# Rotary pairs exchanged by DMA, and the delta rule's chunk inverse with T as transposes of two heads

## The reference

```python
# delta rule, per chunk (kernel: chunks of 128, so that each has two 64-row halves)
m = where(strict, einsum('ik,jk->ij', kb, kc) * decay, 0)
t_mat = triangular_solve(eye + m, eye)                 # inverse of a unit lower triangular matrix
u = t_mat @ vb - (t_mat @ (kb * exp(gcum))) @ state
o = (qc * exp(gcum)) @ state + ((qc @ kc.T) * decay) @ u
state = state * cd + kd.T @ u
# retention: rotary position on q and k, then causal scores with a decay
x * cos(phase) + rotate_every_two(x) * sin(phase)      # rotate_every_two: (-x2, x1) for each pair (x1, x2)
o_ret = ((q @ k.T) * d_mat) @ v
```

## Time and profile before

| | |
|---|---|
| median of 3 runs | 1973.21 us (1970.41 to 1974.37) |
| profiled execution | 1973.4 us |
| its span | 1971.1 us |
| TensorE busy | 1950.8 us, 99% |
| VectorE, ScalarE, GpSimd busy | 1034.0, 757.2, 89.3 us |
| mean granted clock of TensorE | 0.995 |

### The profile page before, as it was taken

One profiled execution on the slowest core, in us unless ns is written; L12 is line 12 of the kernel. 1 busy time (PEld: TensorE's weight loads), 2 busy tenths in 40 slices (PEclk: granted clock), 3 DMA queues, 4 the chain that ended last, 5 costly groups with the idle time before them and its releaser, 6 DMA issues.

```text
span 1971.1 us, 26542 instructions
## 1 busy us (share of the span) xinstructions
PE 1950.8 (99%) x10157; PEld 1558.7 (79%) x10157; DVE 1034.0 (52%) x1416; ACT 757.2 (38%) x936; POOL 89.3 (5%) x81
## 2 busy tenths in 40 slices
PE   8999999999999999999999999999999999999999
PEld 6778888888888788877888888887777788888887
DVE  7745655676447667565543334236668454323433
ACT  5472243445324344443432124134555443212312
POOL 0020210100000010000100000020000010000001
PEclk9999999999999999999999999999999999999999
DMA  6222012232332243212332232342322032223221
GB/s 231 85 88 83 27 36 73 86 101 75 102 107 85 67 139 106 70 59 68 104 107 85 88 104 85 106 126 84 102 80 84 22 107 95 97 85 106 85 93 56
DMA packets 146166, 176.95 MB, mean 90 GB/s; under 512 B 3485, under 2 KB 140317, under 8 KB 143904
## 3 DMA queue, kind: packets, MB, share of 16 engines
q1 hardware_dynamic: 143008, 160.44, 24.9%
q0 software_dynamic: 2784, 15.06, 2.5%
q10 hardware_dynamic: 288, 0.26, 0.0%
HBM read 173.55 MB, written 2.20 MB: 89 GB/s over the span
## 4 chain that ended last, share of the span: by engine, by line
PE 96%; DVE 2%; ACT 1%; issue 0%; DMA 0%; DVEq 0%; ACTq 0%
PE bank L806 28%; PE bank L807 28%; PE bank L808 28%; PE bank L927 3%; PE bank L1394 2%; PE bank L1411 1%; PE bank L961 1%; PE bank L933 1%; PE bank L921 1%; DVE w_lo L1491 1%; PE bank L1215 1%; PE bank L1268 1%; PE bank L969 1%; PE bank L1007 0%; PE bank L999 0%
## 5 line engine op out<-in xcount | busy, mean ns | idle before, releaser
L806 PE MATMUL bank<-n_hi,w_hi 128*128 128x512 f32 x1504 | 612.0, 407 | 7.5 <-DVE w_lo L1507 6.4
L807 PE MATMUL bank<-n_lo,w_hi 128*128 128x512 f32 x1504 | 597.8, 398 | 0.0
L808 PE MATMUL bank<-n_hi,w_lo 128*128 128x512 f32 x1504 | 592.8, 394 | 0.0
L1486 ACT ACTIVATE w_hi<-raw 128x2048 fp32r<-128x2048 f32 x152 | 291.3, 1916 | 766.7 <-PE bank L808 764.3
L1491 DVE TENSOR_TENSOR w_lo<-raw,w_hi 128x2048 fp32r<-128x2048 f32 x152 | 349.3, 2298 | 282.6 <-ACT w_hi L1486 280.7
L806 PEld LDWEIGHTS bank<-n_hi,w_hi 128*128 128x128 f32 x1504 | 283.0, 188 | 85.0 <-issue 15.3
L806 PE MATMUL bank<-ff_hi,w_hi 128*128 128x512 f32 x848 | 338.1, 399 | 3.7 <-DVE ff_lo L2543 2.1
L807 PE MATMUL bank<-ff_lo,w_hi 128*128 128x512 f32 x848 | 338.0, 399 | 0.0
L808 PEld LDWEIGHTS bank<-n_hi,w_lo 128*128 128x128 f32 x1504 | 282.7, 188 | 67.6
L807 PEld LDWEIGHTS bank<-n_lo,w_hi 128*128 128x128 f32 x1504 | 283.2, 188 | 66.7 <-issue 5.3
L808 PE MATMUL bank<-ff_hi,w_lo 128*128 128x512 f32 x848 | 334.6, 395 | 0.0
(11 more groups left out here) (334 smaller groups left out, 1529.4 us busy)
## 6 DMA issues: line engine op xcount, KB each, us to landing
raw<-in_mlp_w_in SPq DMA_DIRECT2D x32, 1024.0 KB, 5.5
raw<-in_mlp_w_out SPq DMA_DIRECT2D x32, 1024.0 KB, 4.9
raw<-in_w_up SPq DMA_DIRECT2D x22, 1024.0 KB, 5.1
raw<-in_w_units SPq DMA_DIRECT2D x14, 1024.0 KB, 4.5
raw<-in_a_w_qkv SPq DMA_DIRECT2D x12, 1024.0 KB, 5.2
raw<-in_b_w_qkv SPq DMA_DIRECT2D x12, 1024.0 KB, 5.2
b_bias<-bias_table POOLq DMA_DIRECT2D x16, 448.0 KB, 4.7
raw<-in_w_down SPq DMA_DIRECT2D x8, 768.0 KB, 4.2
```

Of the source, the lines that this page charges most:

```text
L806: nc.tensor.matmul(b[:, :], w_hi[:, j % 2, cols], hi, start=start, stop=False)
L807: nc.tensor.matmul(b[:, :], w_hi[:, j % 2, cols], lo, start=False, stop=False)
L808: return nc.tensor.matmul(b[:, :], w_lo[:, j % 2, cols], hi, start=False, stop=final)
L1486: act.activation(w_hi[:, s, :], raw[:, s, :], ACT.Copy).then_inc(hi_ready, 1)
```

## The change

1. **Pairs by DMA.** The turn matrix goes; sine has its sign by the row's parity. GpSimd issues four DMAs that copy odd to even rows and even to odd rows of the queries' and keys' tiles into `turned`, now `proj[:, 24:32]`. GpSimd's cosines go; VectorE does sine, cosine and sum of all 8 tiles, 4 before the copies of `p_ret[2]` and 4 behind them (`rotated`).
2. **T by transposes.** In levels 1 to 5 a chunk's T is two full 128x128 transposes, each of two heads' blocks of both halves (`corners_turned`). So T of head h comes to lie in the rows of half h % 2, and so must P. From level 2 on, P and Z are issued for two chunks in two banks, with all four 64x64 tiles (`crossed_products`). In level 6 P goes to the rows by h % 2, and Z is issued crossed.
3. **Order.** T of chunks 2 and 3 moves behind P of chunks 0 and 1 of the next level. The key-query products move from before `p_ret[3]` into levels 1 to 4; values 0 and 1 are transposed within `p_ret[3]`, keys 0 behind A0. In the state loop the four scores are spread: one before u, one behind it, two behind ds. ScalarE's split of weights and its gates move behind T of levels 3 and 4. `g_Y` moves to the buffer of `g_X`, and the copies to it wait until the blocks are placed.

```diff
@@ the ring's list
-        for name in ("gram", "qk"):
-            ring += [(name, c) for c in range(TOK)]
-        ring += [("rot", n) for n in range(4)]
-        ring += [("A0", c) for c in range(TOK)]
+        ring += [("gram", c) for c in range(TOK)] + [("vt", 0), ("vt", 1)]
+        ring += [("A0", c) for c in range(TOK)] + [("kt", 0)]
...
-        LEVEL_BESIDE = {1: [("kt", 0), ("rot", 4)], 2: [("kt", 1), ("rot", 5)], 3: [("kt", 2), ("rot", 6)],
-                        4: [("rot", 7), ("vt", 0)], 5: [("vt", 1)], 6: [("vt", 2), ("vt", 3)]}
+        LEVEL_BESIDE = {1: [("qk", 0)], 2: [("kt", 1), ("qk", 1)], 3: [("kt", 2), ("qk", 2)],
+                        4: [("qk", 3)], 5: [("vt", 2)], 6: [("vt", 3)]}
@@ mixer_pool
+            for half in range(2):
+                group_left(pool, p_ret[half], 1)
+                pool.wait_ge(at("l2_scaled"), 4 * half + 4)
+                for row in range(2):
+                    pool.dma_start(turned[row::2, 4 * half:4 * half + 4, :], proj[1 - row::2, 16 + 4 * half:20 + 4 * half, :]).then_inc(
+                        at("pairs_turned%d" % half), 16)
@@ TensorE
+        def crossed_products(pe, name, n, two, parts, cols, lhsT, rhs):
+            b = [ring_group(pe, (name, n, 2 * two + k)) for k in range(2)]
+            for c in (2 * two, 2 * two + 1):
+                for pair in range(2):
+                    for i, (h, half) in enumerate(parts):
+                        h += 2 * pair
+                        if name == "P":
+                            k, rows = half, HALVES[h % 2]
+                        else:
+                            k, rows = h % 2, HALVES[half]
+                        at0 = (2 * (c % 2) + pair) * cols
+                        ins = nc.tensor.matmul(b[k][rows, at0:at0 + cols], lhsT(c, h, half), rhs(c, h, half), start=True, stop=True)
+                        if c % 2 and pair and i >= len(parts) - 2:
+                            ring_filled(ins)
...
+            for pair in range(2):
+                ins = nc.tensor.transpose(b[:, pair * P:(pair + 1) * P], src[:, 2 * pair:2 * pair + 2, :].rearrange("p h d -> p (h d)"), ident)
@@ mixer_tensor
                 for c in range(TOK):
+                    if c == 2 and n > 1:
+                        corners(n - 1, (2, 3))
...
+                            two_taken(pe, "Z", n - 1, c)
+                            crossed_products(pe, "P", n, c // 2, ((0, 0), (1, 1), (1, 0), (0, 1)), SIDE // 2,
+                                             lambda c, h, half: g_m[HALVES[half], c, h, HALVES[half]],
+                                             lambda c, h, half: odd_blocks(g_Y[:, c], n)[HALVES[half], h])
...
+                        two_taken(pe, "P", n, c)
+                        two_taken(pe, "T", n - 1, c)
+                        rows_of_T = lambda c, h, half: g_T[HALVES[h % 2], c, h // 2 * 2 + half, :]
+                        if n < last:
+                            crossed_products(pe, "Z", n, c // 2, ((0, 0), (1, 0), (0, 1), (1, 1)), SIDE // 2, rows_of_T,
+                                             lambda c, h, half: g_P[HALVES[h % 2], c, h // 2 * 2 + half, 0:SIDE // 2])
...
+                    corners(n, (0, 1))
...
+                retention_scores(pe, c, (1,))
                 ring_taken(pe, ("vt", c))
...
-                retention_scores(pe, c)
+                retention_scores(pe, c, (0,))
...
+                retention_scores(pe, c, (2, 3))
                 pe.wait_ge(at("qd_ready"), c + 1)
@@ VectorE
+        def rotated(dve, half):
+            dve.wait_ge(at("pairs_turned%d" % half), 32)
+            for n in range(4 * half, 4 * half + 4):
+                q = proj[:, 16 + n, :]
+                dve.tensor_tensor(turned[:, n, :], turned[:, n, :], const("sin"), ALU.mult)
+                own_dve(dve, dve.tensor_tensor(q, q, const("cos"), ALU.mult))
+                done(dve, dve.tensor_tensor(q, q, turned[:, n, :], ALU.add), at("rope_done"), n + 1)
...
+            rotated(dve, 0)
             copies(dve, p_ret[2], 24, lambda: grams_vector(dve))
-            key_queries_vector(dve)
+            rotated(dve, 1)
             first_inverse(dve)
-            copies(dve, p_ret[3], 28, lambda: turned_vector(dve, range(4)), leave=True)
+            copies(dve, p_ret[3], 28, lambda: [values_beta(dve, c) for c in range(2)], leave=True)
```

More of the change, by code:

```diff
@@ L275, in build @@
             ("a_pT", [P, 4, SEQ], F32))
[L277 removed]
+        spent = CONST_AT["far_lower"][0]
         a_vn = consts[:, spent:spent + 15 * P].rearrange("p (c d) -> p c d", c=5)
@@ L526, in build @@
         BANKS.update({name: tuple(range(8)) for name in MIXER_RING})
-        BANKS.update({("rot", n): tuple(range(8)) for n in range(4, 8)})
+        BANKS.update({("qk", c): tuple(range(8)) for c in range(TOK)})
+        BANKS.update({key: (4, 5, 6, 7) for key in (("vt", 0), ("vt", 1), ("kt", 0))})
         BANKS.update({key: (4, 5, 6, 7) for key in [("A0", c) for c in range(TOK)] + [("ro", 2), ("ro", 3)]})
@@ L566, in ring_taken, with two_taken, two_chunks @@
             eng.wait_ge(free, before + 1)
+        def two_taken(eng, name, n, c):
+            for k in range(2):
+                ring_taken(eng, (name, n, c // 2 * 2 + k))
+        def two_chunks(v, two, k):
+            return v[:, 2 * two:2 * two + 2, k::2, :].rearrange("p c x d -> p (c x) d")
         def banks_left(eng, banks, key):
@@ L982, in grams, with key_queries, values_turned_first, retention_scores @@
                 four_products(pe, ("gram", c), lambda h: chunk(4 + h, c), lambda h: chunk(4 + h, c))
[L984 to L995, removed]
+        def key_queries(pe, c):
+            four_products(pe, ("qk", c), lambda h: chunk(4 + h, c), lambda h: chunk(h, c))
+        def values_turned_first(pe):
+            pe.wait_ge(at("silu_v"), 1)
+            for c in range(2):
+                four_transposes(pe, ("vt", c), lambda h: chunk(8 + h, c))
+        def retention_scores(pe, h, parts):
             pe.wait_ge(at("rope_done"), 8)
-            for j in range(TOK):
+            for j in parts:
                 b = ring_group(pe, ("rs", h, j))
@@ L1050, in mixer_tensor @@
                 if n < last:
-                    for c in range(TOK):
-                        ring_taken(pe, ("Z", n, c))
-                        side_turned(pe, ("T", n, c), g_Y[:, c], HALVES if n < last - 1 else HALVES[0:1])
+                    corners(n, (0, 1))
             for c in range(TOK):
@@ L1846, in retention, with side @@
                 ring_done(act, act.activation(proj[:, 16 + h, :], b[:, :], ACT.Copy), ("ro", h))
-            def side(b, rows, cols=4 * SIDE):
-                return b[rows, 0:cols].rearrange("p (h d) -> p h d", h=4)
+            def side(b, rows, n=4):
+                return b[rows, 0:n * SIDE].rearrange("p (h d) -> p h d", h=n)
             def key_decayed(c):
```

151 lines of the change are left out of this document (70 added, 81 removed).

## The result

| | before | changed kernel |
|---|---|---|
| runs, median | 1971.81 us (1969.93 to 1974.37, 4 runs) | 1954.32 us (1952.93 to 1956.53, 4 runs) |
| profiled execution, time and span | 1973.4 and 1971.1 us | 1953.94 and 1951.4 us |
| instructions of TensorE | 10157 | 9893 |

The ratio is 0.9909, with a 95% interval of 0.9896 to 0.9923: 17.5 us faster between the medians. Forecast were 11.9 us. Of the 7.2 us, 5.6 are gain that was not forecast; the other 1.6 come from the starting point, a profiled execution of 1973.4 us where the median of the four runs before is 1971.81.

What follows compares the result with a forecast made beforehand. TensorE, 96% of the chain, was taken as the bound. A0 6.05 us earlier, then levels 29.56, waits 0.4 and level 6 4.3, put the inverse's first product 11.9 earlier: 1973.4 - 11.9 = 1961.5 us, range 1957.5 to 1968.

Steps and rivals of the forecast that it cites:

- Ahead of the inverse: Last projection up to level 1: turn and key-query products leave, values' transposes enter; A0 starts 6.05 us earlier, at 211.96.
- The wait of 0.25 us: Head of level 1: TensorE, ready at 214.4, waits 0.25 us for VectorE's last copy of the projection, at 214.65.
- The exchange by DMA: Pairs copied SBUF to SBUF on GpSimd's queue before the rotations: costs 0 us, with 4 kept as possible lateness.
- both of my bounds: First DMA pair: at double the row's 5.2 us it costs nothing; at four times it lands 4 us late.
- T as transposes: Levels of the inverse: T in four chunks falls from 1.90 to 1.16 us, two excursions of 0.58.
- My 0.14 us: Price of TensorE going from 64x64 tiles to 128 and back, 0.58 less 0.44; 10 excursions for T, 1.4 us.
- The levels: Levels 1 to 5 of the inverse: P and Z keep instruction counts at 29.5 ns each; 29.56 us together.
- rival 1: P and Z of levels 2 to 5: crossed tiles take turns at 61 ns, +16.1, in all 1977.6 us; chance 0.03.
- Rival 2: Inverse: the clock falls to half, tile instructions about 53 ns, +18 and +10 us, so 1989; chance 0.03.
- Rival 3: Level ends, head of level 1 or first exchange: waits eat part of the gain, 1963.5 to 1968.5 us; chance 0.25.
- Rival 4: Inverse: switches cost less, level 6 runs at 3.5, no waits: -14 us, 1959.5; chance 0.08.
- The state loop: Behind the inverse: reordered scores remove a wait of 0.38 us but bring three of 0.15; sum 0.

Runs made afterwards that it cites:

- behind_z: The changed kernel with the group beside each level moved behind Z, in front of T of the first two chunks; 1954.68 us, ratio 0.9912.
- eight_in_turn: The changed kernel with the 32 instructions of each crossed two-chunk group sorted by tile, eight in succession on each; 1972.08 us.
- pairs_alone: The kernel before with only the exchange of pairs by DMA, key-query products and inverse as before; 1968.37 us, ratio 0.9978.
- t_by_products: The changed kernel with T as crossed 64x64 products with the identity, 32 per two chunks, in place of four full transposes; 1960.17 us.
- old_inverse: The changed kernel with P, T and Z as before: two tiles, T by products, one bank per chunk; 1963.83 us, ratio 0.9965.

## Why the prediction was right in sign and too small

Point by point, by its own steps:

- **Ahead of the inverse**: right. A0 was forecast at 211.96 and came at 212.04. The queue of VectorE was right as well: its last copies end at 214.45 (forecast 214.65), in its timeline

```profile
213.03 1.42 DVE L2419 TENSOR_TENSOR proj<-bank,rstd 128x512 f32<-128x512 f32 x2
```

  and level 1 starts at 214.64 (forecast 214.65). The wait of 0.25 us there did not show, though: A0 took 2.02 to the transposes (212.04 to 214.06) in place of 1.90, so TensorE was busy up to 214.64. That it came out even is luck: the 0.12 belong to a price that the sum lacks, below.
- **The exchange by DMA**: right at nothing. The transfers' row, issue to landing:

```profile
proj<-proj POOLq DMA_DIRECT2D x4, 512.0 KB, 3.6
```

  They were issued at 159.6 and 170.8; 3.6 us is under the 5.2 of the nearest row, so both of my bounds were too high; VectorE began the rotations at 170.25 and 193.31 without waiting.
- **T as transposes**: right as far as it goes. Four, with the way back to 64x64, take 0.59 us. The Trainium skill (TensorEngine Tiling, "Key Properties") says that a change of tiling mode drains the engine. My 0.14 us, 0.58 less four transposes, is only the part that falls behind the switch. The part ahead of it stands in the interval of the 64x64 group before: in level 1, which is not crossed, P takes 1.99 us and Z 1.98 (214.64 to 216.63, 217.72 to 219.70) where I had 1.88. The trace of before had it too; this is the row that follows the last one of the earlier trace rows there:

```profile
236.74 0.66 PE L927 MATMUL bank<-consts,proj 128*128 128x128 f32 x4
```

  From 234.80 that is 1.94 us for 64 instructions. An excursion costs some 0.2 to 0.25 us, not 0.14; the missing part made level 1 longer than forecast (5.65 against 5.36). In `behind_z` T behind a group of full size takes 0.53.
- **The levels, "P and Z keep their instruction counts"**, costed at 29.5 ns each: this is the step that failed. On four tiles in turn they cost about 15 ns each. From the head of level 1 to the score product I had 34.26 us and it was 30.51, and 3.75 is the whole error at the end of the inverse (248.9 forecast, 245.15 measured). By level, forecast and measured: 5.36 and 5.65; 6.38 and 5.43; 6.38 and 5.44; 5.94 and 5.04; 5.50 and 5.05; 4.3 and 3.90; and 0.4 of waits that in the measured column lie inside. Levels 2 to 5, the crossed ones, came 3.24 us shorter than forecast; level 6 gives 0.40 and the waits 0.40 more, and level 1 takes 0.29 back. P lost 0.34 in each of two groups per level, 0.68. Z took some 0.9 us less for itself, but only 0.27 of that (1.61 in place of 1.88 to the head of T) arrived in level 2. The other part came back as the waits for VectorE, 1.3 us in the view of waits and 0.6 more in level 5 as "issue", where VectorE scales the values (238.82 to 239.95) ahead of the subtraction that T needs. I had those waits, but at 0.4: the parts that I named for the chain through VectorE add up to 0.90, not 0.94, and once Z is short the chain, not TensorE, sets the time to T.
- The error of thought: I read in the earlier trace rows that one tile gives 61 ns and two give 29.5, used it for level 6 ("29.5 ns are possible") and did not go on to four tiles, which the diff names for levels 2 to 5. The only effect of crossing that I priced for these levels was a danger, rival 1. The Trainium skill (TensorEngine Tiling, "Key Properties") says that different tiles load weights and multiply in parallel, and the same page ("The Solution") gives 64x64 as four independent tiles. Put beside the two rows it would have made 15 ns, which the trace and the experiments now show.
- **Rival 1** (turns among crossed tiles): did not come; neither this order nor shared rows slowed them. My argument against it was wrong, though: at 32 columns strict turns should have given about 30 ns, and `eight_in_turn`, at 32 columns, took 42 ns per instruction (1.35 us for 32). **Rival 2** (the clock falls in the inverse): did not come in the changed kernel, 1.00 from 211 to 246, but it did in `pairs_alone`, 0.50 from 221 to 227, and Z took 54 ns per instruction there, near the 53 of the rival. The Trainium skill (TensorE: Matmul & The Clock Gate, "PE-mode transpose") pointed to a fall with T as transposes; with 40 transposes for T among the instructions, none came, and the fall that was seen stands in a kernel with T as products. **Rival 3** (waits): happened, 2.1 us in the view of waits where 0.4 was put in, and was outweighed. **Rival 4** (the change brings more) is what came, but for a reason that it did not list, and larger: 3.75 us at the end of the inverse beyond the forecast, where it had 2.
- **The state loop**: right at about nothing. The wait of 0.38 is gone and the ScalarE waits of 0.15 did not come:

```profile
258.77 1.06 PE L935 MATMUL bank<-g_S,proj 128*128 128x128 f32 x8
```

- **What was not in the sum**: the clock behind the state loop. 2.8 of the 19.5 us between the two profiled executions come from it, and no run tells whether they belong to the change. I took "the later stages are unchanged" as equal time, and built on a profile in which they were at 0.57 for 8 us.

Together: 11.9 forecast, plus 3.75 in the inverse, most of it from the pace, makes 15.7 by the trace; the rest up to the 17.5 between the medians, 1.8, lies in stages that the change does not touch and is of the size by which the executions differ there.

## What to carry to other kernels

Before costing small matmuls, tabulate pace against how many distinct tiles are in turn, and carry the row on to the number that the change will use: tiles times pace was constant here (61, 59 and about 60 ns). Price a change of tile size by the interval of the group ahead of it as well as by its own. When an engine's group gets shorter, the wait that it used to cover comes out: price what follows against the engine that has to answer, and put independent work there rather than ahead. Where two profiles differ in an untouched stage, repeat the same program before giving that difference to the change. And don't read what an edit costs from one total: the trace says where the microseconds lie.

## What the runs showed of the hardware

- One 64x64 fp32 instruction holds its tile for about 60 ns, worked out from the paces: one, two and four tiles in turn give 61, 29.5 and about 15 ns per instruction. Two and four tiles were seen with 32 and with 64 columns, at the same pace; one tile in steady turns only with 64. Four in succession on one tile cost next to nothing (0.63 against 0.60 us for 32), eight cost 0.75 us (1.35 us for 32).
- An excursion from 64x64 to 128x128 and back costs 0.06 to 0.1 us in the interval ahead (1.94 to 1.99 us for 64 instructions in place of 1.88) and 0.14 behind.
- Many such instructions in succession, 32 for T beside 32 for P, brought four standstills of 0.5 to 2.0 us that no other engine explains (`t_by_products`, 4.6 us in all); with T as transposes there were two of 0.45 and 0.24 us.
- The granted clock behind the state loop fell to 0.50 in one execution of a program and stayed at 1.00 in another, with the same instructions.
- Within the inverse the clock fell to 0.50 from 221 to 227 in `pairs_alone`, right after TensorE had waited 1.14 us, and 64 instructions on two tiles took 3.44 us in place of 1.88; in `old_inverse`, which has no such wait, it stayed at 1.00.
